# Row squares shared with VectorE in the first stage, and the gated stage's products as seven block products, in a two-layer mixer kernel

## The reference

```
mod = silu(c) @ mod_w + mod_b                     # shift and scale among six parts
h = rmsnorm(x, g) * (1 + scale) + shift           # the context likewise
...
g = gelu(y)                                        # y: result of the S5 scan, 512 x 1024
ga, gb = split(g @ w_glu, 2, axis=-1)              # w_glu: 1024 x 2048
x = x + gate * (ga * sigmoid(gb))
h = rms_norm(x, norm) * (1 + scale) + shift        # input of the last feed-forward
```

## Time and profile before

| | before |
|---|---|
| median of three runs | 3534.92 us |
| the profiled execution, its own time | 3533.48 us |
| its span | 3531.7 us |
| mean granted TensorE clock | 0.975 |
| TensorE busy | 3230.3 us, 91% |
| VectorE busy | 1600.1 us, 45% |
| ScalarE busy | 638.7 us, 18% |
| moved by DMA | 690.45 MB, mean 196 GB/s |

### The profile page before, as it was taken

How to read it: one execution, slowest core, us unless ns; L and a number is a source line. 1 busy time by engine, 2 the same in 40 slices (tenths; PEclk the granted TensorE clock), 3 DMA queues, 4 the chain that set the end, 5 groups by cost and what they waited for, 6 DMA issues and landing times. The chain is left out here.

```text
span 3531.7 us, 51256 instructions
## 1 busy us (share of the span) xinstructions
PE 3230.3 (91%) x22109; PEld 1826.7 (52%) x22109; DVE 1600.1 (45%) x2891; ACT 638.7 (18%) x1253; POOL 8.6 (0%) x40
## 2 busy tenths in 40 slices
PE   6988999898997988999899899999999987999998
PEld 3567887444444332333333234445688535468853
DVE  3555656446934000100010033663677775157777
ACT  2134332111212000000000031133221003121100
POOL 0000000000000000000000000000000000000000
PEclk9989999899997999999999999999999998999999
DMA  6143435312544999999999942110223355222233
GB/s 246 59 141 127 170 135 185 112 60 42 188 153 159 430 430 430 430 430 428 431 427 428 430 160 88 48 48 31 75 85 106 137 163 226 72 72 91 77 137 131
DMA packets 203126, 690.45 MB, mean 196 GB/s; under 512 B 31256, under 2 KB 96268, under 8 KB 176661
## 3 DMA queue, kind: packets, MB, share of 16 engines
q1 hardware_dynamic: 201912, 686.81, 50.1%
q10 hardware_dynamic: 989, 0.36, 0.0%
HBM read 664.30 MB, written 22.83 MB: 195 GB/s over the span
## 5 line engine op out<-in xcount | busy, mean ns | idle before, releaser
L2305 PE MATMUL banks<-weight_ring,xe_T 128*64 128x512 f32 x1312 | 296.8, 599 | 41.4 <-DMA weight_ring<-in_exp_w 39.3
L3065 PE MATMUL banks<-token_sums,unit_sums 128*128 128x256 f32 x960 | 213.7, 379 | 0.0
L2305 PEld LDWEIGHTS banks<-weight_ring,xe_T 128*64 128x64 f32 x1312 | 90.3, 137 | 235.1 <-issue 160.1
L3065 PEld LDWEIGHTS banks<-token_sums,unit_sums 128*128 128x128 f32 x960 | 182.4, 190 | 24.8
L2321 PE MATMUL banks<-weight_ring,hid_T 128*64 128x512 f32 x656 | 146.7, 596 | 9.6 <-DMA weight_ring<-in_exp_w 9.6
L3065 PE MATMUL banks<-h_T,weight_ring 128*128 128x256 f32 x640 | 151.2, 379 | 0.0
L3291 DVE TENSOR_TENSOR products_kept<-products_kept,banks 128x256 f32<-128x256 f32 x280 | 111.7, 418 | 78.4 <-PE banks L3065 67.6
L2642 PE MATMUL banks<-h_T,weight_ring 128*128 128x512 f32 x320 | 142.1, 597 | 0.0
L3283 DVE SCALAR_TENSOR_TENSOR conv<-products_kept,cols,conv 128x511 f32<-128x511 f32 (+1 forms) x160 | 120.1, 750 | 46.6 <-ACT conv L3174 42.3
L3065 PEld LDWEIGHTS banks<-h_T,weight_ring 128*128 128x128 f32 x640 | 121.6, 190 | 17.4 <-issue 1.0
L2305 PE MATMUL banks<-h_T,xe_T 128*64 128x512 f32 x464 | 105.4, 596 | 17.7 <-DMA h_T<-in_exp_w 17.7
(11 more groups left out here) (682 smaller groups left out, 5386.4 us busy)
## 6 DMA issues: line engine op xcount, KB each, us to landing
weight_ring<-in_exp_w SPq DMA_DIRECT2D x123, 2048.0 KB, 15.7
h_T<-in_exp_w SPq DMA_DIRECT2D x41, 2048.0 KB, 15.7
weight_ring<-in_ada_w SPq DMA_DIRECT2D x24, 2048.0 KB, 8.7
weight_ring<-in_ffn_w_up SPq DMA_DIRECT2D x44, 1024.0 KB, 6.4
weight_ring<-in_ffn_w_down SPq DMA_DIRECT2D x20, 2048.0 KB, 7.7
expert_out<-in_exp_w SPq DMA_DIRECT2D x19, 2048.0 KB, 19.0
weight_ring<-in_mod_w SPq DMA_DIRECT2D x12, 2048.0 KB, 7.9
spare<-in_exp_w SPq DMA_DIRECT2D x9, 2048.0 KB, 20.5
```

Of the source, the lines that this page charges most:

```text
L2305: mm = pe.matmul(k.ps[64 * half:64 * half + 64, 2 * c + b % 2, :], R.rows[:, e // 2 % 2, kt, (e % 2) * CAP:(e % 2 + 1) * CAP], w[:, r, 512 ...
L3065: mm = pe.matmul(k.ps[:, unit_bank[n], low_tokens], left[:, kt, :], right[:, kt, :], start=kt == 0, stop=kt == 3)
```

## The change

In the load stage the masks are no longer loaded; `front` issues them, behind the fourth modulation chunk, and its end waits for them. The ring has one more place for that one chunk (in `k.hT`), so it is issued without waiting for a used place. x is scaled into a tile of its own. The squares of the four x tiles are made by VectorE with `tensor_tensor_reduce`, those of the context stay on ScalarE, before its third copy. The two context tiles are scaled by ScalarE, behind its fourth copy.

In `s5_glu` the work for a pair of token tiles and a half of the columns (value and gate chunk) is one unit. Its operands are cut in four blocks each, tokens by (tile, half of k) and weights by (half of k, value or gate), and seven products of four matmuls replace the eight of four. VectorE makes four token sums a pair and four weight sums a half, and joins the seven products by seven additions. ScalarE copies the first product. Units are (columns 0, pair 0), (0, 1) and (1, 0). The last, (1, 1), stays in whole products. The turns of tiles 0 and 1 now lie ahead of and between the products of tile 3. ScalarE frees the first chunk after the second product of unit 1, the second after its last join, and the third and fourth after the last product. The banks change with it.

The diff, cut to its core:

```diff
         self.lent.update({i: (steps + SLOTS, steps + 8) for i in self.step_slots})
+        self.front_slot = SLOTS + len(self.lent)
...
             sync.dma_start(k.square[:], I["k_square"]).then_inc(consts_landed, 16)
-            sync.dma_start(k.half[:], I["k_half"]).then_inc(consts_landed, 16)
             sync.dma_start(k.misc[:], I["k_misc"]).then_inc(consts_landed, 16)
             k.ring.load_ahead(sync, 0)
             sync.dma_start(k.x[:], I["x"][0].rearrange("(t p) n -> p t n", p=P)).then_inc(k.rows_landed, 16)
-            sync.wait_ge(consts_landed, 48)
+            sync.wait_ge(consts_landed, 32)
...
         source = lambda u: k.x[:, u, :] if u < LT else context[:, u - LT, :]
         target = lambda u: xn[:, u, :] if u < LT else context[:, u - LT, :]
 
         @block.sync
         def _(sync):
-            sync.dma_start(context, k.I["ctx"][0].rearrange("(t p) n -> p t n", p=P)).then_inc(k.rows_landed, 16)
+            sync.dma_start(context, k.I["ctx"][0].rearrange("(t p) n -> p t n", p=P)).then_inc(k.context_landed, 16)
+            k.ring.lend_front(k.hT[:].rearrange("p j n -> p (j n)"))
+            k.ring.load_ahead(sync, 0)
+            sync.dma_start(k.half[:], k.I["k_half"]).then_inc(k.half_landed, 16)
             k.ring.load_ahead(sync, n_chunks)
+            sync.wait_ge(k.half_landed, 16)
             sync.wait_ge(evac_a, DT)
             sync.wait_ge(evac_v, DT)
...
-            pe.wait_ge(normed, tiles)
+            pe.wait_ge(normed, LT)
+            pe.wait_ge(normed_a, CTT)
...
-            for j in range(n_chunks - 1):
+            for j in range(n_chunks - 2):
                 copy(j)
-            act.wait_ge(k.rows_landed, 32)
-            for u in range(tiles):
-                if u:
-                    act.wait_ge(squares, u)
+            act.wait_ge(k.context_landed, 16)
+            for u in range(LT, tiles):
+                if u > LT:
+                    act.wait_ge(squares, u - LT)
                 act.activation(sqr[:], source(u), ACT.Square, accum_out=ss[:, 0, u:u + 1]).then_inc(squares, 1)
-            act.wait_ge(squares, tiles)
+            copy(n_chunks - 2)
+            act.wait_ge(squares, CTT)
+            act.wait_ge(squares_v, LT)
             act.activation(ss[:, 1, :], ss[:, 0, :], ACT.Sqrt, scale=1.0 / D, bias=k.misc[:, 6:7]).then_inc(rooted, 1)
             copy(n_chunks - 1)
+            act.wait_ge(inverted, 1)
+            for u in range(LT, tiles):
+                act.activation(target(u), source(u), ACT.Identity, scale=ss[:, 2, u:u + 1], bias=0.0).then_inc(normed_a, 1)
             act.wait_ge(factors, 1)
...
+            dve.wait_ge(k.rows_landed, 16)
+            for u in range(LT):
+                dve.tensor_tensor_reduce(out=sqv[:], in0=source(u), in1=source(u), scale=1.0, scalar=0.0, op0=ALU.mult, op1=ALU.add,
+                                         accum_out=ss[:, 0, u:u + 1]).then_inc(squares_v, 1)
+                dve.wait_ge(squares_v, u + 1)
             dve.wait_ge(rooted, 1)
-            link(dve.reciprocal(ss[:, 2, :], ss[:, 1, :]))
-            for u in range(tiles):
+            dve.reciprocal(ss[:, 2, :], ss[:, 1, :]).then_inc(inverted, 1)
+            dve.wait_ge(inverted, 1)
+            for u in range(LT):
                 dve.tensor_scalar(target(u), source(u), ss[:, 2, u:u + 1], None, ALU.mult).then_inc(normed, 1)
...
+    part_bank = {1: 0, 2: 4, 6: 1, 7: 2, 5: 3, 4: 5, 3: 6}
+    order = (1, 2, 6, 7, 5, 4, 3)
+    PARTS, JOINS = 7, 7
+    units = ((0, 0), (0, 1), (1, 0))
+    whole_banks = {2: (1, 2), 3: (3, 7)}
+    turn_banks = ((4, 5), (6, 0), (1, 2), (3, 7))
...
+        asum, wsum, kept = sb("token_sums", [P, 2, 4, 4, P]), sb("weight_sums", [P, 4, 4, 512]), sb("products_kept", [P, 7, 512])
+        m1, u2, u3 = kept[:, 4, :], kept[:, 5, :], kept[:, 6, :]
+        value, gate_in = (kept[:, 0, :], kept[:, 1, :]), (kept[:, 2, :], kept[:, 3, :])
...
+        def token_blocks(p):
+            t0, t1 = slice(2 * p * P, 2 * p * P + P), slice(2 * p * P + P, 2 * p * P + 2 * P)
+            return g[:, 0:4, t0], g[:, 4:8, t0], g[:, 0:4, t1], g[:, 4:8, t1]
+
+        def weight_blocks(n):
+            return weights(n, 0)[:, 0:4], weights(n, 1)[:, 0:4], weights(n, 0)[:, 4:8], weights(n, 1)[:, 4:8]
...
+            k.ring.load_ahead(sync, 0)
...
+            def block_product(i, left, right):
+                for kt in range(4):
+                    mm = pe.matmul(k.ps[:, part_bank[i], :], left[:, kt, :], right[:, kt, :], start=kt == 0, stop=kt == 3)
+                mm.then_inc(parts, 1)
+
+            for u, (n, p) in enumerate(units):
+                a11, a12, a21, a22 = token_blocks(p)
+                if p == 0:
+                    k.ring.wait(pe, 2 * n)
+                b11, b12, b21, b22 = weight_blocks(n)
+                s, before = asum[:, p], JOINS * (u - 1)
+                sums_ready = {0: 1, 1: 5, 2: 5}[u]
+                if u:
+                    pe.wait_ge(taken, u)
+                block_product(1, a11, b11)
+                if u:
+                    pe.wait_ge(joined, before + 1)
+                block_product(2, a12, b21)
+                pe.wait_ge(readied, max(sums_ready, 2 + 4 * n))
+                if u:
+                    pe.wait_ge(joined, before + 2)
+                block_product(6, s[:, 1], wsum[:, 1])
+                pe.wait_ge(readied, max(sums_ready, 3 + 4 * n))
+                if u:
+                    pe.wait_ge(joined, before + 3)
+                block_product(7, s[:, 2], wsum[:, 2])
+                if u:
+                    pe.wait_ge(joined, before + 5)
+                block_product(5, s[:, 0], wsum[:, 0])
+                pe.wait_ge(readied, max(sums_ready, 4 + 4 * n))
+                if u:
+                    pe.wait_ge(joined, before + 6)
+                block_product(4, a22, wsum[:, 3])
+                if p == 0:
+                    k.ring.wait(pe, 2 * n + 1)
+                if u:
+                    pe.wait_ge(joined, before + 7)
+                block_product(3, s[:, 3], b22)
...
+            done = JOINS * (len(units) - 1)
+            pe.wait_ge(joined, done + 2)
+            whole(2, 0)
+            pe.wait_ge(joined, done + 3)
+            whole(2, 1).then_inc(products, 1)
+            pe.wait_ge(joined, done + 7)
+            T.pe_turn(pe, 0, turn_banks[0])
+            whole(3, 0)
+            T.pe_turn(pe, 1, turn_banks[1])
+            whole(3, 1).then_inc(products, 1)
+            follow = first_unit(k, 4, (0, 4))
...
+            then(1, lambda: T.pe_turn(pe, 2, turn_banks[2]))
+            T.pe_turn(pe, 3, turn_banks[3])
             then(3)
...
+            for u, (n, p) in enumerate(units):
...
+                act.activation(m1, k.ps[:, part_bank[1], :], ACT.Copy).then_inc(taken, 1)
+                if u == 1:
+                    act.wait_ge(parts, PARTS * u + 2)
+                    act.sem_inc(k.ring.used, 1)
+                act.wait_ge(joined, JOINS * u + 4)
+                if u:
+                    act.wait_ge(updated, 2 * u)
+                act.activation(sg[:, 1, :], gate_in[1], ACT.Sigmoid).then_inc(gated, 1)
+                act.wait_ge(joined, JOINS * u + 7)
+                if u == 1:
+                    act.sem_inc(k.ring.used, 1)
+                act.activation(sg[:, 0, :], gate_in[0], ACT.Sigmoid).then_inc(gated, 1)
+                if n:
+                    T.act_root(act, 0)
+                    T.act_root(act, 1)
+            act.wait_ge(products, 1)
+            act.wait_ge(updated, 6)
+            act.activation(sg[:, 0, :], k.ps[:, whole_banks[2][1], :], ACT.Sigmoid).then_inc(gated, 1)
+            T.act_shift(act, 0, turn_banks[0])
+            T.act_root(act, 2)
+            T.act_shift(act, 1, turn_banks[1])
+            act.wait_ge(products, 2)
+            act.sem_inc(k.ring.used, 1)
+            act.sem_inc(k.ring.used, 1)
+            act.activation(sg[:, 1, :], k.ps[:, whole_banks[3][1], :], ACT.Sigmoid).then_inc(gated, 1)
+            T.act_root(act, 3)
             for t in range(LT - 2, LT):
-                T.act_shift(act, t, banks(t))
+                T.act_shift(act, t, turn_banks[t])
...
+            def token_sums(p):
+                a11, a12, a21, a22 = token_blocks(p)
+                s = asum[:, p]
+                link(dve.tensor_tensor(s[:, 0], a21, a22, ALU.add))
+                link(dve.tensor_tensor(s[:, 1], s[:, 0], a11, ALU.subtract))
+                link(dve.tensor_tensor(s[:, 2], a11, a21, ALU.subtract))
+                dve.tensor_tensor(s[:, 3], a12, s[:, 1], ALU.subtract).then_inc(readied, 1)
...
+                if n:
+                    dve.wait_ge(parts, PARTS + order.index(5) + 1)
+                link(dve.tensor_tensor(wsum[:, 0], b12, b11, ALU.subtract))
+                dve.tensor_tensor(wsum[:, 1], b22, wsum[:, 0], ALU.subtract).then_inc(readied, 1)
...
+                if n:
+                    dve.wait_ge(parts, PARTS + order.index(4) + 1)
```

(49 more changed lines are left out.)

83 lines of the change are left out of this document (33 added, 50 removed).

## The result

The changed kernel took 3514.91 us (median of 4 runs, 3507.77 to 3521.84), against 3534.83 for the kernel before, run beside it (4 runs, 3531.69 to 3539.43): a ratio of 0.9938 with a 95% interval of 0.9925 to 0.9951. The medians lie 19.9 us apart; by the ratio it is 21.9 us less. Five more runs of the same code on another occasion gave 0.993 (0.9916 to 0.9943), which is 24.8 us less; there the medians lie 27.8 us apart. The profiled execution took 3516.07, with a span of 3514.3 against 3531.7.

What follows compares the result with a forecast made beforehand. TensorE, busy 91% of the span, was taken as the bound, with product time binding the gated stage. Products 10.3 + tail 7.3 + first stage 6.8 = 24.4 us less: 3509.1 profiled, 3510.5 median; range 3505 to 3520.

Steps and rivals of the forecast that it cites:

- Block products: Gated stage: three of four units take seven products instead of eight, 24 fewer matmul instructions at 0.43 us, 10.3 us less.
- The line drawn through two durations: Gated stage, VectorE: 0.69 us for 128x512 and 1.23 for 1024 elements, extended to 2.3 for 2048.
- the spare: Gated stage start: sums ready at 7.6 us, TensorE's two products without sums end at 8.9, leaving 1.3 us.
- Tail: End of gated stage: TensorE goes on at once, last unit ends 18.0 us after the products instead of 25.35: 7.3 less.
- First stage: Modulation stage at the start: transposes start at 40.0 to 41.5 instead of 47.68, taken as 6.8 us less.
- The masks: First stage: 544 KB loaded behind chunk 3, worth 1.36 us at 410 GB/s, or nothing if a hole is left.
- The parts of the first stage: Fourth place (product 3 at about 35.1), squares (root at 36.6 against 43.22), scaling shared by VectorE and ScalarE (transposes 40.0 to 41.5).
- The parameter rows: Load ahead of the first stage: small rows may land up to 1.36 us sooner or not; nothing put into the sum.
- The rival by the clock: Gated stage: pauses between block products keep TensorE at half clock, all three units giving 3583; chance 0.04, half near no change.
- The other rivals: Tail keeps its wait (3518, chance 0.14), first stage gives nothing (3517, 0.07), nothing is left (3534, 0.03).
- The tail kept no wait: Rival at the gated stage's end: a late shift or normed row loses the 7.3 us, giving 3518; chance 0.14.
- The first stage's gain isn't nothing: Rival: fourth chunk or next stage's chunks arrive when they did, so the first stage gives nothing, 3517; chance 0.07.

Runs made afterwards that it cites:

- the first profile: Profiled execution of the changed kernel, no further edit, from the first measurement: 3516.07 us, span 3514.3.
- the repeat: The changed kernel once more, no edit, 5 runs: 3511.22 us (3507.48 to 3514.8), span 3505.7.
- the gated stage alone: Kernel before with only the gated stage of the changed one: 3515.99 us (5 runs), ratio 0.9943.
- the order-only kernel: Kernel before, all 256 matmul instructions kept; VectorE shifts row tile 1 ahead of the wait for the last sigmoid: 3531.25 us (11 runs), ratio 0.9981.
- the six: Profiled executions with the whole new first stage: two of the changed kernel, first stage alone, shorter tail, two with later sums; next stage at 48.6 to 52.4.

## Why the prediction was right, and which of its terms were off

The forecast was 3510.5, from 24.4 us less; by their ratios the two measurements are 21.9 and 24.8 us less, with intervals that overlap. By its own steps:

- **Block products: 10.3 forecast, 9.7 and 10.3 measured** (104.4 in the first profile, 103.8 in the repeat, 104 forecast). Over more executions the products took 114.1, 114.6 and 114.8 us in the old form and 104.4, 103.8, 103.8 and 104.5 in the new: 10.4 between the means. The line drawn through two durations for 128x2048 gave 2.3 us; the row has 2.29. The sums were ready 7.4 us after the start, 7.6 forecast. The two products ahead of them took 9.75, 8.9 forecast: the stretch at half clock was longer than in the earlier trace rows. So the spare was 2.3, not 1.3; in the repeat, where they took 9.2, it was 1.8. How long the clock stands at half there differs from one execution to the next, and the margin with it.
- **Tail: 7.3 forecast, 7.4 measured** in both profiles and in the gated stage alone; last unit at 10.8 and to 17.9 after the products, where 10.8 and 18.0 stood. The mechanism named (a shift queued behind an update that waits) is shown by the order-only kernel, which has 6.9 of it.
- **First stage: 6.8 forecast, 6.3 and 7.6 measured** at the next stage's start, and 7.8 (4.6 to 11.0) in the runs with it alone. The six profiled executions with the new stage start the next one 7.3 us sooner in the mean than the three with the old (50.3 against 57.6); the nearest pair is 4.9 apart, the farthest 9.3, so that the first two lay so close to 6.8 is in part luck. The masks were priced at 0 to 1.36 us, by their bytes, and the fourth product came 1.4 us later behind the first with them ahead.
- **The parts of the first stage** were priced as if each stood alone, and they don't add. Against the mean of the six, the next stage starts 4.1, 4.0 and 3.8 us later when the place, the squares or the order of the masks is taken back, 11.9 in all for a stage that gained 7.3. Two of the parts bring the fourth chunk sooner and one the root, and the transposes wait for both (without the place for ScalarE behind the fourth product, with the squares back for VectorE behind the root), so a gain on one chain alone is lost in the wait for the other. Each of the three is one execution, though, later than the slowest of the six by 1.6 to 2.0 us and with 1.3 to 1.7 us of half clock in its fourth product; whether a part taken back makes that likelier isn't shown.
- **The parameter rows.** The prediction put nothing on their coming sooner, and weighed what the Trainium skill says in "DMA: Bandwidth & Descriptors", "Issuing engines are not separate DMA queues", that transfers of all issuing engines interleave on the same sixteen, by which it worked out a start 1.36 us sooner. The first product starts at 24.9, 25.6, 24.9 and 26.0 with the masks ahead (mean 25.36), and at 24.4 to 25.7 in eight executions with them behind (mean 25.0). That is 0.4 sooner inside a scatter of 1.3: it can't be told from none, and 1.36 isn't seen.
- **The rival by the clock** is refuted for this stage. The granted clock is 1.00 from 2995 to 3089.5, through all units, and behind a pause of 5.6 us it was at 0.51 for 3.3 us and then at 1.00 again. The prediction named a rule by which this rival would be the likely one, from "A second HAM failure mode: psum-queue depth-cycling" of the Trainium skill's page "TensorE: Matmul & The Clock Gate". That section tells of a TensorE that stands idle for moments between its groups of matmuls. Here the banks are cycled too, but TensorE's timeline has no idle time between the block products, so the trace neither shows the swing nor speaks against the page.
- **The other rivals.** The tail kept no wait. The first stage's gain isn't nothing, and what looks like it in the first profile (0.3 us late at the gated stage) is not in the repeat, and goes with a lower granted clock on the way. What stays open is why a given execution gets its full clock sooner in the sparse stages; the runs show only that it differs from one to the next with the same code.

## What to carry to other kernels

Before an arithmetic saving is tried, look at the idle time that ends on an engine's own queue: a step that was ready, issued behind one that waits for the last result, cost 7 us here, and one line of order takes most of it away. Where TensorE bounds a stage, fewer matmuls are worth their count times their time, if the other engine's sums fit into the products that need none; work out that spare, since overrunning it cost the overrun here and, when the wait was 5.6 us and not 0.3, a stretch at half clock. And a short stage's gain in a long program is to be judged by that stage's own rows, and by many runs, not by one pair of spans.

## What the runs showed that I had not expected

- In the first stage the same 16 instructions of 128x512 took 1.92 us in some executions and 3.1 to 3.6 in others. Behind pauses of 0.7 us or less it was always 1.92; behind 1.1 to 2.9 us it was the longer time in six of eight.
- With the 544 KB of masks at the head of the queue SyncE issued x later: at 8.2 to 10.1 us in four executions, against 6.6 to 7.5 in eight with the masks behind, 2.2 us in the mean, 1.6 times their 1.36 us at 410 GB/s. From issue to landing x took 19.4 to 20.1 us either way.
- ScalarE's table load moved ahead of a wait when the activation stood right behind that wait, and stayed behind it with two semaphore increments between: 1.28 us on the chain that ended last, for the order of two lines.
- Executions of one code differ by up to 14 us (3507.48 to 3521.84), which goes with the mean granted clock (0.976 and 0.972).
